# Where the last quarter of an output-projection unit stands against the transposes of the probabilities, in two softmax groups of a hybrid decoder trunk

## The reference, cut to what matters

```python
for i in range(DEPTH):                      # DEPTH = 2
    h = rms_norm(x, attn_norm[i])
    proj = h @ w_in[i]
    o_a = stick_breaking_attn(...)          # group SB
    o_b = causal_softmax_attn(q_m, k_m, v_m)        # group MLA
    o_c = sliding_window_sink_attn(q_c, k_c, v_c, swa_sinks[i])   # group SWA
    o_d = moba_attn(q_d, k_d, v_d)          # group MOBA
    groups = jnp.stack([o_a, o_b, o_c, o_d], axis=2)   # each (B, S, 256)
    groups = rms_norm(groups, group_norm[i].reshape(4, 256))
    x = x + groups.reshape(B, S, 1024) @ w_o[i]
    # then: gated MLP with a causal convolution (2816 wide), then the per-layer embedding
```

## Time and profile before

| | |
|---|---|
| median of 3 runs | 669.44 us (669.35 to 670.4) |
| the profiled execution's own time | 669.66 us |
| its span in the trace | 667.9 us |
| TensorE matmul busy | 658.0 us, 99% |
| VectorE, ScalarE, GpSimd busy | 435.6, 422.0, 404.8 us |
| DMA | 115.18 MB, 172 GB/s over the span |

### The profile page before, as it was taken

The page is one execution under the profiler, slowest core; times in us unless marked ns, Lnnn a source line. Parts: engine busy times, 40 slices in busy tenths (PEclk is TensorE's granted clock), DMA queues, the critical chain, the costliest instruction groups (busy, mean ns, idle before and its releaser), DMA issues.

```text
span 667.9 us, 9533 instructions
## 1 busy us (share of the span) xinstructions
PE 658.0 (99%) x3784; PEld 571.6 (86%) x3784; DVE 435.6 (65%) x619; ACT 422.0 (63%) x629; POOL 404.8 (61%) x216
## 2 busy tenths in 40 slices
PE   7999999999999999999999999999999999999997
PEld 5988988888888888888889889888888888888885
DVE  6977787749898985003488588865689898910033
ACT  6669875776767675334474897747776767643342
POOL 5523500288888887987841163005888888889871
PEclk9999999999999999999999999999999999999999
DMA  9962233675555555553386421155555555555411
GB/s 321 374 227 64 68 123 110 199 247 191 191 190 190 191 190 188 189 189 106 107 297 228 158 95 64 64 190 182 192 189 190 190 189 193 190 190 188 158 31 64
DMA packets 74445, 115.18 MB, mean 172 GB/s; under 512 B 2336, under 2 KB 58272, under 8 KB 74144
## 3 DMA queue, kind: packets, MB, share of 16 engines
q1 hardware_dynamic: 73248, 111.75, 50.2%
q10 hardware_dynamic: 1152, 2.81, 1.2%
HBM read 113.51 MB, written 1.05 MB: 172 GB/s over the span
## 4 chain that ended last, share of the span: by engine, by line
PE 89%; DVE 7%; ACT 2%; DMA 1%; issue 1%; SPq 0%; ACTq 0%
PE ps L1441 24%; PE ps L940 14%; PE ps L942 14%; PE ps L941 14%; PE ps L1443 12%; ACT pb L632 1%; PE ps L1097 1%; PE ps L992 1%; DMA raw<-w_in 1%; DVE st L1685 1%; PE ps L1080 1%; PE ps L954 1%; DVE wl L1901 1%; PE ps L1027 1%; DVE hn L1990 1%
## 5 line engine op out<-in xcount | busy, mean ns | idle before, releaser
L459 POOL TENSOR_TENSOR wl<-raw,wh 128x2048 fp32r<-128x2048 f32 (+1 forms) x74 | 334.3, 4521 | 85.2 <-ACT wh L578 85.2
L1441 PE MATMUL ps<-hT_hl,wh 128*128 128x512 f32 x688 | 238.6, 392 | 0.0
L578 ACT ACTIVATE wh<-raw 128x2048 fp32r<-128x2048 f32 (+1 forms) x102 | 186.2, 1828 | 75.4 <-PE ps L942 68.5
L1443 PE MATMUL ps<-hT_hl,wl 128*128 128x256 f32 x688 | 193.3, 281 | 0.0
L1441 PEld LDWEIGHTS ps<-hT_hl,wh 128*128 128x128 f32 x688 | 129.2, 188 | 28.2
L1443 PEld LDWEIGHTS ps<-hT_hl,wl 128*128 128x128 f32 x688 | 129.4, 188 | 0.0
L446 POOL TENSOR_SCALAR st<-st 128x2 f32<-128x2 f32 (+3 forms) x26 | 11.1, 426 | 124.7 <-ACT lat L643 67.8
L940 PE MATMUL ps<-wh,hT_hl 128*128 128x512 f32 (+1 forms) x220 | 80.9, 368 | 0.0
L942 PE MATMUL ps<-wh,hT_hl 128*128 128x512 f32 (+1 forms) x220 | 79.0, 359 | 0.0
L941 PE MATMUL ps<-wl,hT_hl 128*128 128x512 f32 (+1 forms) x220 | 78.9, 359 | 0.0
L1925 DVE TENSOR_TENSOR x<-x,ps 128x512 f32<-128x512 f32 x16 | 10.8, 684 | 99.5 <-PE ps L942 97.5
(11 more groups left out here) (306 smaller groups left out, 1173.3 us busy)
## 6 DMA issues: line engine op xcount, KB each, us to landing
raw<-w_up SPq DMA_DIRECT2D x44, 1024.0 KB, 5.1
raw<-w_down SPq DMA_DIRECT2D x22, 1024.0 KB, 4.9
raw<-w_in SPq DMA_DIRECT2D x16, 1024.0 KB, 9.2
raw<-w_o SPq DMA_DIRECT2D x6, 1024.0 KB, 4.9
raw<-ple_gate SPq DMA_DIRECT2D x6, 1024.0 KB, 4.8
raw<-w_in SPq DMA_DIRECT2D x4, 704.0 KB, 5.3
ng<-norm_gains ACTq DMA_DIRECT2D x2, 1024.0 KB, 6.6
raw<-w_o SPq DMA_DIRECT2D x4, 512.0 KB, 4.0
```

What stands on the lines that cost most here:

```text
L459: pool.tensor_tensor(wl[:, slot, 0:n], raw[:, slot, 0:n], w_high(u)[:, 0:n].bitcast(F32), ALU.subtract).then_inc(done, 1)
L578: act.activation(w_high(u)[:, c:n], raw[:, slot, c:n], ACT.Copy).then_inc(h_made, 1)
L1441: pe.matmul(both, high[:, c], hU_all[:, k].rearrange("p a n -> p (a n)"), start=k == 0, stop=False, skip_group_check=True)
L1443: mm = pe.matmul(o, wl[:, slot, c], hU_h[:, k, :], start=False, stop=k == KT - 1, skip_group_check=True)
```

## The change

In TensorE's list, in two places of each layer, `project_out(n, (3,))` and `probs_T(n+1)` change places. The six matmuls of quarter 3 now run behind the twelve transposes of the probabilities, and the `w_used` count of units 10 and 11 goes up there. The lists of the other engines, all waits and all data stay as they are.

```diff
                 pe.wait_ge(F["swaT_ready"], base["swaT_ready"] + 6)
                 project_out(0, (2,))
                 group_T(1)
+                probs_T(1)
                 project_out(0, (3,))
-                probs_T(1)
                 pe.wait_ge(F["mix_low"], base["mix_low"] + 2)
                 pv(1, lambda h, k: v_moba[:, k, h * HD:(h + 1) * HD], 7)
                 half_scores(2, ...)
                 project_out(1, (0, 1, 2))
                 group_T(2)
+                probs_T(2)
                 project_out(1, (3,))
-                probs_T(2)
                 pe.wait_ge(F["mix_low"], base["mix_low"] + 3)
                 pv(2, lambda h, k: v_swa[:, k, (h // 2) * HD:(h // 2 + 1) * HD], 7,
                    GROUPED)
```

## The result

The changed kernel takes 670.88 us (median of 22 runs, 670.35 to 673.42) where the kernel before takes 670.09 in the 22 runs timed beside it. These two medians are 0.79 us apart and the means 1.15; the ratio estimated from all the runs is 1.0018 with a 95% interval of 1.0012 to 1.0024, so the change makes the kernel slower by 0.8 to 1.6 us with 1.2 in the middle. The forecast was +1.1 (ratio 1.0016).

The account below looks back on a forecast made before the run. TensorE, busy 99% of the span at a granted clock in the top tenth, was taken as the bound. 2 x 0 for the first swap plus 2 x 0.55 for the second gave 669.44 + 1.1 = 670.5 us, range 669.4 to 671.3.

Parts of the forecast that it names:

- The second swap costs, through the buffer count: Unit 11's late release delays `high(14)`; `low(14)` comes 0.81 later, less 0.31 slack at `group_T(3)`, plus 0.05: 0.55 us a layer.
- the hand-over from the cast to the low part: Between ScalarE's `high(14)` and VectorE's `low(14)` behind the second swap: taken as 0.03 us.
- The two gains are eaten: Second swap: copies start without their 0.44 us wait, products 0.23 earlier; TensorE's gain only lengthens its wait at `group_T(3)`.
- The first swap costs nothing: Group 1: products start when they did, set by the copy behind `group_low(1)`; priced 0, a 0.1 gain eaten at `group_T(2)`.
- The sum: Both layers together: 2 x 0 for the first swap plus 2 x 0.55 for the second, +1.1 us.
- one sign of being wrong: Listed as showing the forecast wrong: the second `group_T` moved from 104.17.
- case 2: Products' earlier start at the second swap counts: 0.23 a layer, -0.46 in all, 669.0 us; chance 0.13.
- case 3: First swap: part 2's wait for the last exponential delays the products past 0.3 slack; total 1.7, 671.1 us; chance 0.13.
- case 4: Sixteen transposes in a row run at 0.216 us each, delaying quarter 3 by 2.59: +3.7, 673.1 us; chance 0.04.

Follow-up runs that it names:

- The count moved by itself: Kernel before with no matmul moved; unit 11's `w_used` count goes up at the eleventh of group 2's twelve transposes, 1.2 us later: ratio 1.0016.
- both runs with a late count: Kernel before, TensorE's order kept, unit 11's count moved to group 2's transposes (ratio 1.0016) or to the middle of its products, 3.4 us later (1.0106).
- the halves: Both swaps, VectorE's low part of unit 14 cut in two around group 3's division: ratio 0.9985 against the kernel before; without the swaps 1.0002.
- both kernels that had the overlap: Low part of unit 14 moved whole behind group 3's division: with both swaps ratio 1.0001, in the order of before 1.0011, against the kernel before.
- the same run: Kernel before, order kept, unit 11's count moved to the middle of group 2's products, 3.4 us later: ratio 1.0106.

## Why the prediction was right

- **The second swap costs, through the buffer count.** Right, and the size nearly so: the cast idle 2.05 us (2.0 forecast), `low(14)` waiting 1.47 (1.2 forecast), the last `group_T` waiting 0.73 (0.7 forecast), 0.58 + 0.06 us a layer with the second swap alone (0.55 forecast). The count moved by itself gives 0.47, and its cast starts 3.34 us behind the second `group_T` (107.55 - 104.21), 0.12 sooner than in the changed kernel (108.25 - 104.79 = 3.46). That is the whole difference to 0.58 within 0.01 us, which leaves nothing for the order of the matmuls. What the forecast had too small is the hand-over from the cast to the low part, 0.03, for which it had no row: it measured 0.10 (108.25 + 1.91 = 110.16, then 110.26), and 0.10 in both runs with a late count too. So the low part came 0.89 later by the second `group_T` (5.47 instead of 4.58) and not 0.81, and 0.89 - 0.31 is the 0.58.
- **The two gains are eaten.** Right. The products start 3.20 us behind the second `group_T` (107.99 - 104.79) instead of 3.42, and the wait behind them takes it back. With the halves it appears as 0.33 us a layer, more than the 0.23 I gave it: products that don't begin out of a wait are also quicker, 2.59 us from the first of them to the next weights' product (107.99 to 110.58) instead of 2.67 (107.59 to 110.26).
- **The first swap costs nothing.** Right in its verdict, wrong in one reading. I held that the first copy waited for `group_low(1)` alone. Without the transposes in front of it, it starts 0.61 us behind that instruction (93.92 to 94.53) instead of 0.68: the last of its first four transposes seems to have held it still by 0.07. And the gain is not eaten by the wait at the second `group_T`, as I wrote, for VectorE's chain, which sets the end of that wait, starts from this very copy. It comes through as 0.10 us a layer.
- **The sum.** -0.10 + 0.58 + 0.06 in place of 0 + 0.55, so +1.1 either way; measured 1.2, between 0.8 and 1.6. That the two agree so closely is partly luck: the second swap cost 0.09 more than forecast and the first gained the 0.10 that was priced at nothing. By the letter one sign of being wrong came true, the second `group_T` moved from 104.17 to 104.79; 0.72 of that was there before the first swap, and without it `group_T(2)` came 0.10 earlier.
- **The rivals.** The gain that counts (case 2) needed `high(14)` through by 108.5; it ended at 108.25 + 1.91 = 110.16, or 109.5 on the clock of the kernel before (0.62 less, by the second `group_T`), 1.0 too late. The first swap as a cost (case 3) is excluded by that swap alone. Slow transposes (case 4): sixteen in a row went from 104.79 to 106.51, 0.108 us each, at a granted clock of 1.00, as the table by stretch of the changed kernel has it:

```profile
104.80:107.70 2.90, 2.90 (x21) 2.72 (x22) 2.54 (x4) 1.40 (x6) 0.00 (x0) 1.00 0.00 0
```

  The TensorE page of the Trainium skill (PE-mode transpose) states that transposes do not raise the clock. These sixteen ran behind matmuls at full clock and it stayed at 1.00; whether transposes would raise a clock that is low, no run here shows.

## What to carry to other kernels

When a block of matmuls is moved, look at what its last one releases: who waits for that count on another engine, and what is queued behind that waiter. Here the low part of weights that TensorE first used at 117.71 (L1309) waited for a late cast and stood, from 110.26 on, ahead of a short chain that TensorE did need. The new order gained only with that low part cut in two around the division, and the halves gained only with the new order. And an instruction put into an engine's idle time is free only if it doesn't hold up a third engine, as the whole low part did here with GpSimd.

## What the runs showed of the hardware

- GpSimd's step on 128x2 elements took 0.19 us alone and 1.22 us when it began inside a VectorE subtraction of two 128x2048 operands in SBUF; it ended 0.05 to 0.06 us behind that subtraction in both kernels that had the overlap. A step on 128x16 that began 0.05 us into such a subtraction took 2.30 and ended 0.06 behind it. With two such different starts the time was the rest of VectorE's instruction, not a slower pace.
- A pause of 2.46 us brought the granted clock of TensorE from 1.00 to 0.50, from about 117.0 to 120.4, and cost 1.10 us besides the pause; after one of 2.48 us in the same run it stayed at 1.00. TensorE was busy at full clock ahead of both. Why only one of them cost the clock is open.
